# A two-part, four-layer network on one core: queries and keys as wide and narrow products, softplus and squares moved, loads in another order

## What is computed

```python
# first part, convolution branch
y = a * jax.nn.sigmoid(g)
y = depthwise_conv(y, conv_dw)            # 31 taps
y = jax.nn.silu(layernorm(y + conv_b, ln_g, ln_b)) @ conv_pw
# second part, mixer
proj = u @ w_in                           # ..., q, k, v, ... are slices of proj
# rg_lru
r = sigmoid(blockdiag(x, w_a) + b_a); i = sigmoid(blockdiag(x, w_x) + b_x)
log_a = -8.0 * r * jax.nn.softplus(-lam)  # lam: one number per channel
a = jnp.exp(log_a)
u = jnp.sqrt(-jnp.expm1(2.0 * log_a)) * (i * x)
h = scan(h * a + u)
# retention
q = rope(q, positions); k = rope(k, positions) / 16
scores = q @ k.T * decay
```

## Time and profile before

| | |
|---|---|
| median of three runs | 2346.39 us (2345.78 to 2347.6) |
| the profiled execution | 2349.3 us |
| its span (first to last instruction) | 2347.4 us |
| TensorE busy | 2316.0 us, 99% of the span |
| VectorE busy | 1535.1 us, 65% |
| ScalarE busy | 1200.5 us, 51% |
| GpSimd busy | 74.6 us, 3% |
| transfers | 435.95 MB, 186 GB/s on average |

### The profile page before, as it was taken

How to read it: one execution, slowest core, us unless ns; L and a number is a source line. 1 busy time by engine, 2 the same in 40 slices (tenths; PEclk the granted TensorE clock), 3 DMA queues, 4 the chain that set the end, 5 groups by cost and what they waited for, 6 DMA issues and landing times.

```text
span 2347.4 us, 30345 instructions
## 1 busy us (share of the span) xinstructions
PE 2316.0 (99%) x12100; PEld 1962.3 (84%) x12100; DVE 1535.1 (65%) x2037; ACT 1200.5 (51%) x1752; POOL 74.6 (3%) x133
## 2 busy tenths in 40 slices
PE   8999999999999999999999999999999999999999
PEld 6788888788888888978888888888889788888887
DVE  6867667766666557776575666665577765856664
ACT  6545456454455455545344555554555553444553
POOL 0100000100000000000000000000000000000000
PEclk9999999999999999999999999999999999999999
DMA  8436656346656556645555465565566455664553
GB/s 293 153 108 216 204 175 224 130 137 222 203 166 225 189 172 205 202 144 181 183 192 197 162 207 192 176 227 189 176 201 204 147 179 180 192 202 162 192 193 127
DMA packets 119804, 435.95 MB, mean 186 GB/s; under 512 B 13552, under 2 KB 13808, under 8 KB 119408
## 3 DMA queue, kind: packets, MB, share of 16 engines
q1 hardware_dynamic: 119664, 434.01, 56.0%
HBM read 432.91 MB, written 1.05 MB: 185 GB/s over the span
## 4 chain that ended last, share of the span: by engine, by line
PE 87%; DVE 7%; DMA 2%; ACT 1%; POOL 1%; issue 1%; SPq 0%; DVEq 0%; POOLq 0%; ACTq 0%
PE ub L1636 21%; PE ub L1640 11%; PE ub L1614 8%; PE ub L1616 8%; PE ub L1615 8%; PE acc L1614 8%; PE acc L1616 8%; PE acc L1615 8%; DVE wlo L975 2%; DMA raw<-in_w 1%; DVE XN L1016 1%; ACT junk L524 1%; DMA tapw<-in_taps 1%; PE acc L2065 1%; PE acc L1950 1%
## 5 line engine op out<-in xcount | busy, mean ns | idle before, releaser
L975 DVE TENSOR_TENSOR wlo<-raw,whi 128x1024 fp32r<-128x1024 f32 x776 | 917.8, 1223 | 246.8 <-ACT whi L502 245.0
L502 ACT ACTIVATE whi<-raw 128x1024 fp32r<-128x1024 f32 x776 | 783.3, 1053 | 264.9 <-PE ub L1616 149.5
L1636 PE MATMUL ub<-xhl,whi 128*128 128x512 f32 x2176 | 595.2, 395 | 0.0
L1636 PEld LDWEIGHTS ub<-xhl,whi 128*128 128x128 f32 x2176 | 375.5, 189 | 53.5 <-issue 1.0
L1640 PEld LDWEIGHTS ub<-xhl,wlo 128*128 128x128 f32 x2176 | 333.5, 189 | 46.1
L1640 PE MATMUL ub<-xhl,wlo 128*128 128x256 f32 x2176 | 345.8, 281 | 0.0
L1614 PE MATMUL acc<-whi,bhl 128*128 128x512 f32 x736 | 288.3, 392 | 0.0
L1616 PE MATMUL acc<-whi,bhl 128*128 128x512 f32 x736 | 287.4, 391 | 0.0
L1615 PE MATMUL acc<-wlo,bhl 128*128 128x512 f32 x736 | 287.2, 390 | 0.0
L1614 PE MATMUL ub<-whi,xhl 128*128 128x512 f32 (+1 forms) x704 | 275.5, 391 | 8.1 <-DVE wlo L975 4.9
L1616 PE MATMUL ub<-whi,xhl 128*128 128x512 f32 (+1 forms) x704 | 272.8, 387 | 0.0
(11 more groups left out here) (298 smaller groups left out, 2442.7 us busy)
## 6 DMA issues: line engine op xcount, KB each, us to landing
raw<-in_w SPq DMA_DIRECT2D x776, 512.0 KB, 4.9
gain<-in_gains SPq DMA_DIRECT2D x20, 512.0 KB, 7.7
tapw<-in_taps SPq DMA_DIRECT2D x16, 512.0 KB, 6.7
par<-in_par SPq DMA_DIRECT2D x2, 1068.0 KB, 9.7
DEC<-in_decay SPq DMA_DIRECT2D x2, 768.0 KB, 8.3
par<-in_par SPq DMA_DIRECT2D x2, 647.0 KB, 6.9
H<-in_x SPq DMA_DIRECT2D x2, 512.0 KB, 4.7
out_h<-H SPq DMA_DIRECT2D x4, 256.0 KB, 2.2
```

The costliest lines, as they stand in the source:

```text
L502: do(act.activation(whi[:, s % RING, c], raw[:, s % RAW, c], ACT.Copy), counts["w_hi"])
L975: do(dve.tensor_tensor(wlo[:, s % RING, c], raw[:, s % RAW, c], whi[:, s % RING, c].bitcast(f32), ALU.subtract), counts["w_lo"])
L1636: pe.matmul(bank, whi[:, s % RING, n:n + P], xhl[:, kt, :, :].rearrange("p a n -> p (a n)"), start=kt == 0, stop=False, skip_group_check=True)
```

## The change

TensorE: q and k chunks use `pair`, with PSUM slot 0 for q and slot 1 for k. ScalarE therefore copies the left halves in each of these steps, and VectorE adds the right halves into `tS` and rotates from there. VectorE's two preparing instructions and `softplus` move into the feed-forward part ahead of the mixer (steps w_down 3 and 5), ScalarE's small exponential with them (w_down 4). The squares of the decays move from VectorE to ScalarE, two instructions of 128 x 1024 at the end of `decays`, written into `XA`. SyncE loads chunk 2 ahead of constants, parameters and a gain, which follow the chunks 5 and 7; in each layer of the first part the tap pieces 5 to 7 are issued ahead of the chunk w_out 3. `gated(1)` comes in round 2 instead of 3. A one-element Silu on ScalarE, with the load of its table, stands ahead of the copy of the second attention half. The diff, without the declaration of `spare` (two numbers, zeroed by GpSimd) and of two semaphores, without the moved text of `softplus`, which is unchanged, and with the wait for `pos_in` lowered by the load that moved:

```diff
@@ SP: order of the loads @@
     load(1)
     sp.dma_start(cst[:, K["freqs"]:], a["consts"][:, K["freqs"]:]).then_inc(sem["pos_in"], 16)
     sp.dma_start(pos1[:, :], a["pos1"]).then_inc(sem["pos_in"], 16)
-    sp.dma_start(posi[:, :], a["pos2"]).then_inc(sem["pos_in"], 16)
+    load(2)
     sp.dma_start(cst[:, P:K["freqs"]], a["consts"][:, P:K["freqs"]]).then_inc(sem["cst2_in"], 16)
-    load_par1(0)
-    load_gain(0, 1)
     for L in range(LAYERS):
         for s in range(s1(L, "inp"), s1(L, "end")):
-            if s >= 2:
+            if s >= 3:
                 load(s)
+            if s == 5:
+                load_par1(0)
+            if s == 7:
+                load_gain(0, 1)
+                sp.dma_start(posi[:, :], a["pos2"]).then_inc(sem["posi_in"], 16)
...
                 load_taps(L, 1, 2)
                 sp.wait_ge(sem["dots_done"], IDX_HEADS * (L + 1))
-                load_taps(L, 2, 5)
-            if s == s1(L, "out", 3):
-                load_taps(L, 5, PIECES)
+                load_taps(L, 2, PIECES)
...
@@ ACT: first part, before attended(1) @@
+        act.wait_ge(sem["spare_ready"], 1)
+        do(act.activation(spare[:, 1:2], spare[:, 0:1], ACT.Silu))
         attended(1)
...
@@ ACT: the second part's ffn(), in a step of w_down @@
                     prep(min(s + 3, s0 + 32))
+                    if (name, j) == ("f1", 4):
+                        nxt("root_in")
+                        do(act.activation(small[:, 2, :], small[:, 1, :], ACT.Exp, scale=-1.0),
+                           counts["root_ready"])
...
@@ ACT: decays() @@
                 do(act.activation(Ag[:, f, :], Rg[:, f, :], ACT.Exp, scale=small[:, 7, f:f + 1]))
             settle()
             for f in range(4 * half_, 4 * half_ + 4):
-                do(act.activation(Rg[:, f, :], Rg[:, f, :], ACT.Tanh, scale=small[:, 7, f:f + 1]),
-                   counts["exd"] if f % 4 == 3 else None)
+                do(act.activation(Rg[:, f, :], Rg[:, f, :], ACT.Tanh, scale=small[:, 7, f:f + 1]))
+            do(act.activation(XA[:, 4 * half_:4 * half_ + 4, 3:], Ag[:, 4 * half_:4 * half_ + 4, :], ACT.Square),
+               counts["exd"])
...
@@ ACT: mixer @@
-            elif (kind, j) == ("q", 0):
+            elif kind in ("q", "k"):
+                slot = 0 if kind == "q" else 1
+                if j:
+                    act.wait_ge(sem["qk_ready"], 8 * L + 2 * j + slot - 1)
+                else:
+                    act.wait_ge(sem["xs"], 4 * L + 3 + slot)
+                sums_out(slot, s, slot)
+            if (kind, j) == ("q", 0):
                 sigmoids(2)
             elif (kind, j) == ("k", 0):
                 sigmoids(3)
-            elif (kind, j) == ("q", 1):
-                nxt("root_in")
-                do(act.activation(small[:, 2, :], small[:, 1, :], ACT.Exp, scale=-1.0), counts["root_ready"])
             elif (kind, j) == ("k", 1):
                 nxt("coef_ready")
                 decays(0)
             elif (kind, j) == ("k", 3):
                 nxt("root_in")
                 do(act.activation(wide(Rg), wide(Rg), ACT.Sqrt, scale=-1.0), counts["root_ready"])
-                act.wait_ge(sem["xs"], 4 * L + 4)
+                act.wait_ge(sem["qk_ready"], 8 * (L + 1))
...
@@ DVE: first part, the top 64 @@
-            if r in (1, 3):
-                gated(r // 2)
+            if r in (1, 2):
+                gated(r - 1)
...
@@ DVE: the second part's ffn(), in a step of w_down @@
+                    if (name, j) == ("f1", 3):
+                        dve.wait_ge(sem["par_in"], 16 * (LAYERS + L + 1))
+                        lam = par2[:, P2["lam"]:P2["lam"] + 8]
+                        do(dve.tensor_scalar(small[:, 0, :], lam, -1.0, 0.0, ALU.mult, ALU.max))
+                        do(dve.scalar_tensor_tensor(small[:, 1, :], lam, -1.0, lam, ALU.mult, ALU.max),
+                           counts["root_in"])
+                    elif (name, j) == ("f1", 5):
+                        softplus()
...
@@ DVE: mixer, kind q or k @@
                 dst, slot = (q2, 0) if kind == "q" else (k2, 1)
-                used(s)
+                x = units(tS[:, slot, :])
+                sums(slot, slot, x, "pd")
                 settle()
-                bank = units(ub[:, 2 * slot, :])
-                do(dve.tensor_tensor(units(tX[:, 0, :]), bank, cos_sin, ALU.mult))
-                do(dve.tensor_tensor(units(tX[:, 1, :]), bank, sin_cos, ALU.mult), counts["pd"])
+                do(dve.tensor_tensor(units(tX[:, 0, :]), x, cos_sin, ALU.mult))
+                do(dve.tensor_tensor(units(tX[:, 1, :]), x, sin_cos, ALU.mult))
                 settle()
                 do(dve.tensor_tensor(dst[:, 2 * j, :], tX[:, 0, 0:S], tX[:, 0, S:], ALU.subtract))
                 do(dve.tensor_tensor(dst[:, 2 * j + 1, :], tX[:, 1, 0:S], tX[:, 1, S:], ALU.add),
                    counts["qk_ready"])
-                if (kind, j) == ("q", 1):
-                    softplus()
-                elif (kind, j) == ("k", 1):
+                if (kind, j) == ("k", 1):
                     dve.wait_ge(sem["sigs"], 8 * (L + 1))
                     settle()
                     do(dve.tensor_tensor(wide(Ig), wide(Ig), wide(Cg), ALU.mult))
                 elif (kind, j) == ("k", 2):
                     dve.wait_ge(sem["exd"], 2 * (L + 1))
                     settle()
-                    do(dve.tensor_tensor(wide(Cg), wide(Ag), wide(Ag), ALU.mult))
-                    settle()
-                    do(dve.scalar_tensor_tensor(wide(Rg), wide(Cg), 1.0, wide(Rg), ALU.add, ALU.mult),
+                    do(dve.scalar_tensor_tensor(Rg[:, :, :], XA[:, :, 3:], 1.0, Rg[:, :, :], ALU.add, ALU.mult),
                        counts["root_in"])
...
@@ PE: mixer, kind q or k @@
-                slot = 0 if kind == "q" else 1
-                fill(U_[2 * slot], "pd")
-                for f in range(2):
-                    arrive(s, f)
-                    for kt in range(KT):
-                        last = tile(ub[:, 2 * slot, f * S:(f + 1) * S], xhl[:, kt, :, :], s, f * KT + kt,
-                                    kt == 0, kt == KT - 1)
-                give(last)
+                pair(s, 0 if kind == "q" else 1, "pd")
```

57 lines of the change are left out of this document (28 added, 29 removed).

## The result

The changed kernel takes **2353.25 us**, the median of 10 runs (2351.16 to 2355.75); the kernel before, beside it, 2347.97 (10 runs, 2345.78 to 2350.92). The ratio is 1.0023, 95% interval 1.0015 to 1.0031: 5.3 us slower. The prediction was 2345.6 us with a range of 2338 to 2352. The change of 0.23% lies just over the 0.2% that the prediction called no change, on the side that it gave 0.12.

A forecast was written before the change was run, and what follows sets the result against it. TensorE, busy for 99% of the span, was taken as the bound. The first part's -5.6 us and the second's +4.8 summed to -0.8, giving 2345.6 us against the median of 2346.39, with a range of 2338 to 2352.

The forecast's parts named there:

- start: Kernel start: loading chunk 2 earlier removes TensorE's 1.10 us wait for its split, -1.2 us.
- taps: Convolution taps: earlier loads remove the wait and slow clock, -3.2 us in the second layer, -0.4 in the first.
- gate: Gated block one round earlier: pooling starts 0.4 us earlier on GpSimd, 0.4 us saved per layer, -0.8 us.
- first part together: Start, taps and gate terms of the first part summed, -5.6 us.
- second part: Mixers: ScalarE's and VectorE's queues delay TensorE, +2.4 us a layer, +4.8 us, TensorE's savings included.
- the first part gives less: Rival: w_out 3 loads later or the clock falls anyway, late parameters cost; -2.4 instead of -5.6, 2348.8 us; chance 0.14.
- mixer's chain: Mixer, q 1 to first scores: full ScalarE and VectorE queues make TensorE wait at k 3, g 0 and first scores.
- Nothing more is lost: Mixer behind the first scores: product and decayed scores done near 1017.7, needed at 1018.2, so no further loss.
- square and the table load: ScalarE's queue in the mixer: a 128x1024 square takes 1.0 us, a table load 1.28 us.
- a table switch costs twice: Rival: ScalarE also stands still during each table load, 1.28 us; +2.6, 2348.2 us; chance 0.03.
- The clock falls in the mixer: Rival: the clock falls after both 1.8 us waits in both layers, 5.6 us on top, 2351.2 us; chance 0.12.
- anchor: The kernel before's median, 2346.39 us, to which the forecast's sum was applied.

The follow-up runs named there:

- start_only: Kernel before with only the order of the loads at the start changed; 2346.80 us, ratio 0.9996.
- taps_only: Kernel before with only the taps' loads changed, all issued right behind the dots; 2347.95 us, ratio 0.9999.
- gate_only: Kernel before with only the gated block one selection round earlier; 2349.65 us, ratio 1.0008.
- first_only: Kernel before with the first part's edits alone (start loads, taps, gated block, early Silu); 2348.15 us, ratio 1.0003.
- before_again: Kernel before, unchanged, profiled a second time; 2348.58 us.
- pair_only: Kernel before with only queries and keys as wide and narrow products, softplus and squares staying where they were; 2357.11 us, ratio 1.0038.
- second_only: Kernel before with the second part's edits alone (wide and narrow products, softplus moved, squares on ScalarE); 2354.65 us, ratio 1.0029.
- fixABGL: Against fixAB: gated block back in its old round, VectorE's first weight-split pair one head later; 2345.99 us, ratio 0.9992.
- halves: Against fixAB: gated block back in its old round, VectorE's three weight-split pairs cut in six, one behind each of six heads; 2343.21 us, ratio 0.9980.
- fixAB: Kernel after with VectorE's wide product behind the last key's rotation and the second half of the decays one chunk later; 2346.22 us, ratio 0.9992.

## Why the prediction was wrong

The terms, with what each came to:

| term | forecast | measured | by |
|---|---|---|---|
| start | -1.2 | -1.0 | start_only |
| taps | -3.6 | -0.1 | taps_only |
| gate | -0.8 | +1.6 | gate_only |
| first part together | -5.6 | +0.2 | first_only |
| second part | +4.8 | +5.5 | ruler |
| median of before | 2346.39 | 2347.97 | 10 runs |

- **The taps' term failed**, and it was the largest. Its step was "wait and slow clock go: 1.8 + 1.5" (the wait is 1.72 by its row), read from one execution. In other executions the clock falls 5 to 6 us earlier, at a wait that the edit leaves alone, and the taps' wait is mostly small or missing (not there at all in before_again). Taken away, it makes room for the wait for `work` or changes nothing. The prediction had this in the rival "the first part gives less" (the clock falls all the same), at -2.4, still too much.
- **The gate's term had the wrong sign.** The step "pooling starts 0.4 us earlier, I take 0.4 per layer" had two faults. The row says that one addition took 1.05 us, not two, and it did get shorter (0.60 in gate_only), but the instruction ahead of it took 0.85 us instead of 0.36, so VectorE came out no earlier, and TensorE, there sooner, just waited longer (1.06 us against 0.34). And the step did not look at what VectorE does next: a pair of splits ahead of the second head's scores, which now met the whole of GpSimd's subtraction of 128x512, 3.96 us against 3.42.
- **The start's term held**: -1.0 by medians, about -1.5 by the moment at which TensorE is ready for `YT`. Its bound used 1.4 MB for the loads put off; they are 1.3 MB, or 1.6 with p, so 3.5 to 4.2 us at 377 GB/s. Nothing rested on it.
- **The mixer's chain held**: forecast waits 0.6, 1.8 and 1.8 us, measured 0.67, 1.75 and 1.56. Counted from the first part's last wait, the first scores began 2.6 us later (119.82 - 117.21), forecast 2.4. "Nothing more is lost" behind them was off by some 0.15 a layer. The forecast's additions are rounded up: three chunks from 979.4 end at 996.2, not 996.0, and its own rows added up give 1011.0 for the last key, not 1011.4, which is 2.0 us a layer instead of 2.4. The agreement to 0.2 us is partly owed to that. From the copy of k 1 to the first scores it was 32.26 us, forecast 32.1.
- **The square and the table load held**: the square took 1.04 us, forecast 1.0; the table load 1.28, and the exponentials began 0.02 us behind it. So the rival "a table switch costs twice", 2348.2 us, falls. The Trainium skill (ScalarE: Activation LUTs, What ACT_TABLE_LOAD costs) has a drain with each switch, which by its figure gave 2348.4; the trace doesn't agree, 0.02 us against 1.38.
- **"The clock falls in the mixer"** did not happen in three profiles with waits up to 1.76 us. It did in pair_only, at waits of 3.65 and 3.66 us. The rival with the right sign for the time had the wrong place: the falls are in the first part.
- **The anchor**: 2346.39 us was the median of three runs; in later groups the kernel before came to 2347.8 to 2348.5. The profiled execution at 2349.3 warned that single executions lie some us apart, and I said that it changes nothing in the differences. It did, since the wait and slow clock that I then counted as the edit's gain are part of what that execution had on top.

2345.6, with 1.6 for the anchor, 5.8 for the first part and 0.7 for the second added, is 2353.7, and 2353.25 was measured. The first part's +0.2 is known to about 2 us only. That after is 1.4 us faster than second_only, which differs from it in the first part alone, hints that it is worth a little more there.

## What to carry to other kernels

A wait or a slow clock in one profile is a gain only if it is in the next profile too: take two of the kernel as it is, and compare the place before pricing it. Before adding work to engines that are nearly in the way, write down their queue from the first shared buffer on and look for the one long instruction that can stand behind the critical ones; here moving one 2.29 us product, with what hangs on it, and ScalarE's second half of the decays turned a loss of 5.5 us in the second part into a gain of 2.3. Where another engine's long pieces make a wait that the clock answers to, cutting them in two can be worth more than moving them: moved, the wait and the slow clock came along (fixABGL), cut, neither was there (halves).

## What the runs showed of the hardware

- The wait for the scaled scores, 1.93 to 2.49 us among small matmuls, stands in 17 of the profiles. In their 34 passes the granted clock went to 1.2 GHz at it in 18 (from 0.4 us before its end to 1.4 us behind it) and in 16 it did not. A fall lasts 3 to 4 us and makes the stretch from `YT` to the group means about 1 us longer (31.4 to 31.6 against 30.1 to 30.8, with the gate where it was and no wait for taps). With waits of 0.8 us at most it did not fall in the one profile of halves. That the cuts prevent the fall rests on that profile, on the 2.1 us of the medians and on the clocks of the 11 executions. Why it falls in one pass and not in the next with the same wait stays open.
- ScalarE loads its table ahead of the wait of the instruction that needs it: in fixAB the load for the square root ran at 1004.94 us, and the square root itself began at 1009.27, when its input came. The table switch in front of this wait cost nothing:

```profile
1004.94 1.28 ACT L926 ACT_TABLE_LOAD   x1
1009.27 1.92 ACT L926 ACTIVATE Rg<-Rg 128x2048 f32<-128x2048 f32 x1 [3.04 <-DVE Rg L1524]
```

- GpSimd and VectorE slow each other by an amount that depends on how they meet: the same pair of splits took 2.35, 3.42 and 3.96 us, the same four products on GpSimd 3.26 and 4.18. GpSimd's subtraction of 128x512 took 2.13 us beside the pair and 1.27 in fixABGL, where the pair came behind it.
